# Hybrid decoder block on one core: the up product of the shared expert's first 256 remaining rows, made ahead of the last routed expert's down products

## The reference

```python
def swiglu(t, wg, wu, wd):
    return (jax.nn.silu(t @ wg) * (t @ wu)) @ wd
...
        moe = swiglu(t, ws_gate[i], ws_up[i], ws_down[i]) + routed_experts(t, w_router[i], router_bias[i], we_gate[i], we_up[i], we_down[i])
        h = layer_norm(ALPHA * h + moe.reshape(b, l, d), ln2_g[i], ln2_b[i])
    return h[:, N_META:]
```

## Time and profile before

| | us |
|---|---|
| median of 3 runs | 3154.47 |
| lowest and highest run | 3150.10, 3158.81 |
| profiled execution | 3153.83 |
| its span, first to last instruction | 3152.0 |
| TensorE busy (share of span) | 3090.0 (98%) |
| VectorE busy | 1105.2 (35%) |
| ScalarE busy | 686.5 (22%) |
| GpSimd busy | 641.7 (20%) |

### The profile page before, as it was taken

How to read it: one execution, slowest core, us unless ns; L and a number is a source line. 1 busy time by engine, 2 the same in 40 slices (tenths; PEclk the granted TensorE clock), 3 DMA queues, 4 the chain that set the end, 5 groups by cost and what they waited for, 6 DMA issues and landing times.

```text
span 3152.0 us, 38064 instructions
## 1 busy us (share of the span) xinstructions
PE 3090.0 (98%) x14302; PEld 1990.3 (63%) x14302; DVE 1105.2 (35%) x3389; ACT 686.5 (22%) x1553; POOL 641.7 (20%) x631
## 2 busy tenths in 40 slices
PE   8999999999999999999999999999999999999997
PEld 4445555554445555554556767877787777878775
DVE  6422433330026766763777411111111111111115
ACT  2311111110014455541111011111111111111114
POOL 3300000000000110111454212222222223232325
PEclk9999999999999999999999999999999999999999
DMA  6421010001000103006434567887888888888886
GB/s 224 154 70 28 14 28 14 1 14 59 15 7 6 50 11 108 11 8 219 151 124 152 181 215 229 231 242 237 242 245 240 241 242 264 263 266 269 273 239 237
DMA packets 179112, 458.82 MB, mean 146 GB/s; under 512 B 24944, under 2 KB 97472, under 8 KB 153192
## 3 DMA queue, kind: packets, MB, share of 16 engines
q1 hardware_dynamic: 133872, 339.23, 30.4%
q0 software_dynamic: 42752, 108.72, 15.7%
q10 hardware_dynamic: 2304, 8.39, 0.7%
HBM read 342.33 MB, written 113.92 MB: 145 GB/s over the span
## 4 chain that ended last, share of the span: by engine, by line
PE 53%; DVE 1%; POOL 0%; issue 0%; ACT 0%; ACTq 0%
PE ps L2362 23%; PE ps L2304 11%; PE ps L2170 7%; PE ps L2288 4%; PE ps L2218 3%; PE ps L2301 2%; PE ps L2230 1%; PE ps L2190 1%; PE ps L2248 0%; PE ps L2180 0%; POOL moe_fin L1971 0%; PE ps L2157 0%; DVE moe_fin L1636 0%; PE ps L2203 0%; PE ps L2202 0%
## 5 line engine op out<-in xcount | busy, mean ns | idle before, releaser
L697 PE MATMUL ps<-ret_w,hT 128*128 128x512 f32 (+1 forms) x1088 | 465.0, 580 | 0.0
L2362 PEld LDWEIGHTS ps<-moe_xT,moe_wg 128*128 128x128 f32 x2048 | 352.7, 196 | 44.8 <-issue 40.8
L2362 PE MATMUL ps<-moe_xT,moe_wg 128*128 128x192 f32 (+22 forms) x2048 | 378.4, 338 | 0.0
L2362 PE MATMUL ps<-moe_xT,moe_wu 128*128 128x192 f32 (+22 forms) x2048 | 375.2, 336 | 0.0
L2304 PE MATMUL ps<-moe_wd,moe_hh 128*128 128x512 f32 (+12 forms) x800 | 366.5, 601 | 1.0 <-DVE moe_hh L1454 0.8
L2362 PEld LDWEIGHTS ps<-moe_xT,moe_wu 128*128 128x128 f32 x2048 | 353.3, 196 | 4.3
L1912 POOL DMA_INDIRECT base_rows<-moe_yo,index x100 | 164.8, 1648 | 847.4 <-DVE moe_yo L1559 717.4
L697 PEld LDWEIGHTS ps<-ret_w,hT 128*128 128x128 f32 (+1 forms) x1088 | 195.5, 185 | 223.0 <-issue 215.9
L1454 DVE TENSOR_TENSOR moe_hh<-moe_sl,ps 128x256 f32<-128x256 f32 (+19 forms) x144 | 53.8, 373 | 771.2 <-ACT moe_sl L2026 765.5
L2304 PEld LDWEIGHTS ps<-moe_wd,moe_hh 128*128 128x128 f32 (+12 forms) x800 | 136.6, 181 | 159.3 <-issue 149.8
L1057 PE MATMUL ps<-hT,fox_w 128*128 128x512 f32 (+1 forms) x576 | 228.5, 558 | 0.0
(11 more groups left out here) (251 smaller groups left out, 3589.5 us busy)
## 6 DMA issues: line engine op xcount, KB each, us to landing
moe_wg<-in_we_gate SPq DMA_DIRECT2D x64, 1024.0 KB, 4.9
moe_wu<-in_we_up SPq DMA_DIRECT2D x64, 1024.0 KB, 7.0
moe_wd<-in_we_down SPq DMA_DIRECT2D x64, 1024.0 KB
fox_c<-ck SPq DMA_DIRECT2D x8, 1032.0 KB, 8.7
emb_xin<-in_x SPq DMA_DIRECT2D x16, 512.0 KB, 3.9
h_rows<-emb_hr SPq DMA_DIRECT2D x16, 512.0 KB, 2.9
ret_w<-in_w_in SPq DMA_DIRECT2D x16, 512.0 KB, 6.6
moe_yt<-h_rows SPq DMA_DIRECT2D x16, 512.0 KB, 4.9
```

Of the source, the lines that this page charges most:

```text
L697: ins = pe.matmul(ps[0:n, g % 2, lo:hi], hT[:, c, t0:t0 + n], wr[u][:, c, lo:hi], start=(c == 0), stop=(c == DC - 1))
L2362: ins = pe.matmul(out, w[:, c, f:FF:FC], xT[u][:, c, 0:n], start=(c == 0), stop=(c == DC - 1))
```

## The change

The up product `tail_up(0)` is made between the last routed expert's up products and its down products. ScalarE's silu and VectorE's product for it move with it, to a place directly behind those of the last routed expert and ahead of that expert's evictions. In front of the overflow branch TensorE gets a wait for the hidden rows of the moved product. Nothing is added or taken away besides that, and the lists of GpSimd and SyncE are the same.

```diff
@@ VectorE @@
                 product(SH + i, c, lambda f: ps[:, 2 + f, 256:256 + c] if c <= 256 else ps[:, 4 + f, 0:c])
+                for f in (range(FC) if i == NE - 1 else []):
+                    tail_product(0, f)
...
-            tail_product(0, 0)
             moments(0)
             moments(1)
             moments(2)
-            tail_product(0, 1)
             moments(4)
@@ ScalarE @@
                 silu(SH + i, CAPS[i])
+                if i == NE - 1:
+                    silu(SH + NE, SW)
...
-            tail_silu(0, 0)
             act.wait_ge(all_added, 1)
             nc.scalar.copy(wide(ps[:, 0:2, :]), brow2[:, :]).then_inc(rows_set, 1)
-            tail_silu(0, 1)
             moments(0)
@@ TensorE @@
                     ins.then_inc(gu, 1)
+                if i == NE - 1:
+                    tail_up(0)
...
+            pe.wait_ge(hd, FC * (SH + NE + 1))
             overflow(pe, n_over, extra_block)
-            tail_up(0)
             tail_up(1)
             tail_down(0)
```

## The result

| | before | after |
|---|---|---|
| median, us (7 runs each) | 3150.1 | 3162.15 |
| lowest and highest run | 3149.0, 3158.81 | 3161.15, 3165.69 |
| profiled execution | 3153.83 | 3161.15 |
| its span | 3152.0 | 3159.3 |

The ratio is 1.0033, with a 95% interval from 1.0024 to 1.0043: slower by some 10 us (8 to 14), near the edge of what a measurement of this kernel can tell.

A forecast was written before the change was run, and what follows sets the result against it. Bound taken: the closing chain from the last scatter through tile loads and GpSimd's row additions back to TensorE. 13.98 − 0.76 − 0.45 − 1.06 + 0.9 = +12.6 us on 3153.83 gave 3166.4 us; range 3158 to 3172.

The forecast's parts named there:

- The moved product, +13.98: On TensorE: 64 records of L2218 now precede the down products the last scatter needs, delaying them by 13.98 us.
- the removed wait, −0.76: On TensorE in front of L2304: the wait for the last expert's hidden rows goes, saving 0.76 us.
- The issue gap behind the branch, 0: TensorE's 1.66 us gap behind the branch was let stand; bounds −1.66 and +1.66, showing only if TensorE sets the pace.
- The first load of a sum, +13.22: On SyncE: the first load of a sum is issued 13.22 us later, at 3093.68 instead of 3080.46.
- Slack of the first group, −0.45: On ScalarE: measuring the fourth tile starts when it lands, no longer behind the moved product's activation, saving 0.45 us.
- the others follow, 1.29 us apart: Tile loads after the first: the tiles behind it were claimed to land 1.29 us apart, as in the kernel before.
- Slack on GpSimd, −1.06: GpSimd's first eight row additions: its two stops, 0.62 and 0.44 us, go and the additions run without a stop.
- TensorE's new wait and its clock, +0.9: First tail down products: TensorE stops about 10.7 us, restarts at half clock; 0.1 to 1.9 reaches the end, 0.9 taken.
- DMA at nothing: Loads and stores at the end move together, and the third product's rows arrive in time, so DMA costs nothing.
- TensorE alone: Rival: TensorE alone sets the end, only the removed wait shows, 3153.1 us, not slower; chance 0.10.
- TensorE's restarted stream as the pace: Rival: TensorE's restarted stream, not GpSimd, sets the pace at the end; +10.0, 3163.8 us; chance 0.15.
- A long low clock: Rival: TensorE's half clock lasts 13.7 us from the restart, delaying the third up product; +15.6, 3169.4 us; chance 0.08.

The follow-up runs named there:

- experiment 2: Kernel before, nothing moved, with 7 of 8 of the first tail up product's matmuls left out; 84.57 us from last expert's second activation to end, ratio 0.9994.
- experiment 9: Kernel before with 2 of the product's 32 matmuls ahead of the last expert's down products, the rest behind the branch; 89.95 us in the profile, ratio 1.0002.
- experiment 3: Changed kernel with the third tail product's rows loaded behind all 16 tiles instead of behind the twelfth; 98.58 us, ratio to before 1.0036.
- experiment 5: As experiment 4, with the wait for the moved product's hidden rows taken from in front of the branch into the skipped body; 88.35 us, ratio 1.0007.
- 6: As experiment 5, with 2 of the product's 32 matmuls ahead of the last expert's down products, the other 30 behind them; 88.37 us, ratio 1.0005.
- 7: Changed kernel with its added wait in the skipped body instead of in front of the branch; 98.42 us, ratio to before 1.0037.
- experiment 8: Changed kernel with four extra matmuls, results unused, in TensorE's stop ahead of the second half of the first tail down products; 98.24 us, ratio to before 1.0044.
- experiment 1: Changed kernel with only the first half of the product ahead of the last expert's down products, the second half behind the branch; 89.87 us, ratio 1.0009.
- 10: Kernel before with 8 of the product's 32 matmuls ahead of the last expert's down products; 86.28 us, ratio 0.9995.
- experiment 4: Changed kernel with the moved product behind the last expert's down products but still ahead of the branch; 94.62 us, ratio 1.0025.

## Why the prediction was right, and where it was not

The forecast was 3166.4 us, +12.6 on the profiled execution. From A the trace has +11.95. The median came out at 3162.15, inside the range, and 4.2 below the forecast, nearly all of which is the base: the kernel before had 3150.1 over seven runs, where the forecast stood on one execution of 3153.83. The medians differ by 12.05; the ratio gives 10.4.

- *The moved product, +13.98, and the removed wait, −0.76.* Right in kind: the last scatter is issued 12.79 us later instead of 13.22. The groups of records overlap at their ends, so the product takes 13.82 us from its start to that of L2304, and the removed gap is 0.92 counted the same way (together 12.90); the down products ran 0.1 us tighter.
- *The issue gap behind the branch, 0.* It went (−1.66), the lower of the two bounds, but as said it shows only where TensorE sets the pace, and it did not.
- *The first load of a sum, +13.22.* It was +11.76, 0.43 of the miss by the item above. The step that failed for the rest is "ScalarE's two evictions and GpSimd's two scatters follow the down products as before": from scatter to load took 5.92 instead of 6.95. The two runs with a code load about 3 us ahead of the first tile load have the long value (before 6.95, experiment 2 6.61), all others 5.7 to 6.1, among them experiment 9 (6.09) with a code load 1.1 us ahead. The connection is by this comparison alone and the cause stays open.
- *Slack of the first group, −0.45.* It was +1.18, and this is the step that failed most: "the others follow, 1.29 us apart". VectorE waited 2.30 us for the fifth tile. In all six runs with a code load 6.0 to 6.2 us behind the first tile load (after, 3, 5, 6, 7, 8) ScalarE's statistics began 8.9 to 9.1 us after it, waiting for the fourth tile. In the five without one there they began at 7.5 to 7.7 where ScalarE waited for the tile (1, 2, 10), and at 7.9 and 7.7 where it came from other work (before, 4), so the tile was there by then. In experiment 9 other work came first, at 12.28. Experiment 3 took away my first explanation; this one rests on the comparison of runs, none of which placed a code load on purpose.
- *Slack on GpSimd, −1.06.* Right, −0.94: its two stops went as described, but for the 0.17 that the half clock left.
- *TensorE's new wait and its clock, +0.9.* The wait came (13.11 us where 10.7 were expected, in part because the gap of 1.66 ahead of it had gone) and the restart was at 0.50, as the rows of windows below show, with the second half at 5.42 us instead of 3.6. The size was wrong: experiment 8 puts it under 0.2. GpSimd had 1.6 us in hand, as worked out; of the two bounds, 0.1 and 1.9, the lower was right, since the low clock ended 3.5 us after the restart.

```profile
3097.60:3100.40 2.80, 0.00 (x0) 0.00 (x0) 1.50 (x3) 1.51 (x5) 1.07 (x2) 1.00 1.03 418
3100.50:3114.10 13.60, 3.47 (x4) 1.51 (x5) 11.56 (x25) 12.79 (x19) 7.67 (x8) 0.50 1.05 352
3114.20:3116.20 2.00, 2.00 (x7) 1.02 (x6) 0.80 (x2) 2.00 (x3) 2.00 (x2) 1.00 0.99 399
```

By the Trainium skill ("TensorE: Matmul & The Clock Gate", What's actually happening) activity releases the throttle. The trace agrees: the clock falls to 0.50 within the stop, is back at 1.00 after TensorE has worked again for 3.5 us, and from 3115.88 on 64 records of L2218 take 13.98 us as before.

- *DMA at nothing.* The tiles and the third product's rows did not disturb each other (experiment 3: 98.58 us against 98.31). But the fourth tile came later, in the runs with a code load among the tiles, and code loads had not been thought of.

So three mis-sized terms (−1.46 on the first load, +1.63 on the first group, −0.7 on the clock) left an error of 0.65 us. That the sum came out better than its parts is luck.

Of the rivals, *TensorE alone* fell with experiment 2 (−1.8 for 12.2 us of work). *TensorE's restarted stream as the pace* (+10.0) fell on GpSimd's row: 0.17 us of stop in its first eight additions. *A long low clock* did not happen: 3.5 us from the restart, not 13.7. (Its "twice" is twice 6.8 us; rows 7 show 6 of that stretch.)

## What to carry to other kernels

A busy share of 98% did not mean that moving TensorE's work is free: work at the end of a program should not stand ahead of what the last DMA chain needs, here the down products whose scatter releases the loads. Up to the slack of that chain, here 1.4 us, it is free (a quarter of the product), beyond it each us costs one. A branch with an unmet wait in front of it, at a moment when the DMA engines are full, cost 6.3 us more than the same wait in the skipped body. A stop costs more than its length where TensorE sets the pace: in experiments 4, 5 and 9 the half clock behind it added 2.8, 1.8 and 2.9 us.

## What was not expected of the hardware

A code load of 16 KB some 6 us behind the first tile load went with a fourth tile some 1.4 us later, in six of six runs and in none of the five without, at an unchanged rate of the DMA. TensorE waited up to 7.29 us for code behind a branch in experiment 4, and up to 3.63 elsewhere, with nothing in its rows but "issue". The queue for instructions tells it: in all six runs with such a stop (before, 2, 4, 5, 6, 9) TensorE went on 1.2 to 1.6 us after a 16 KB load on that queue had ended. Stops as short as 1.99 us (experiment 1) and 2.13 (experiment 5) had 3.4 us at half clock behind them. What part of the code each load carries, and for which engine, the traces do not say.
